# Routing of one prompt block moved in among another block's value tokens, and the cache key units re-dealt 20, 15, 25, 4

## The reference, cut to what matters

```python
q = einsum('td,de->te', xb, w_peer_q)                 # 1024 -> 8 heads x 2 x 128
s = einsum('thpc,hpkc->thpk', q, peer_sub_keys)       # 16 lists of 128 scores
top_s, top_i = top_k(s, 16)                           # per list, then the best 16 of 256 pairs
u = peer_u[expert]                                    # 8 heads x 16 rows of 1024 floats per token
act = gelu(einsum('thkd,td->thk', u, xb))
y = einsum('thk,thkd->td', gate * act, peer_v[expert])
```

## Time and profile before

| what | value |
| --- | --- |
| three runs | 2271.04, 2278.25, 2282.62 us |
| median | 2278.25 us |
| profiled execution, its time | 2283.16 us |
| its span, first to last instruction | 2281.3 us |
| TensorE busy | 1697.5 us (74%) |
| VectorE busy | 1131.0 us (50%) |
| GpSimd busy | 1239.4 us (54%) |
| ScalarE busy | 360.3 us (16%) |
| moved by DMA | 784.77 MB, mean 344 GB/s |
| of it the gathers (GpSimd's queue) | 547.43 MB |
| and SyncE's and ScalarE's transfers (q1) | 231.08 MB |

### The profile page before, as it was taken

One profiled execution on the slowest core, in us unless ns is written; L12 is line 12 of the kernel. 1 busy time (PEld: TensorE's weight loads), 2 busy tenths in 40 slices (PEclk: granted clock), 3 DMA queues, 4 the chain that ended last, 5 costly groups with the idle time before them and its releaser, 6 DMA issues.

```text
span 2281.3 us, 32035 instructions
## 1 busy us (share of the span) xinstructions
PE 1697.5 (74%) x11231; PEld 718.0 (31%) x11231; DVE 1131.0 (50%) x2727; ACT 360.3 (16%) x761; POOL 1239.4 (54%) x1076
## 2 busy tenths in 40 slices
PE   8999898783788767789999777787666223237878
PEld 2455776440112433333334333331212000011212
DVE  2553798988504776482006676780000455550362
ACT  1222243210000222221213222310000000000000
POOL 0000174667777768556668788665233544554765
PEclk9999987897999978899999888899888555557999
DMA  5005495899999999999999999999999999999998
GB/s 226 23 21 186 144 349 184 318 354 346 379 406 394 399 344 398 397 357 399 400 398 390 397 399 399 399 375 368 402 402 401 409 404 404 404 395 368 357 338 330
DMA packets 258555, 784.77 MB, mean 344 GB/s; under 512 B 36593, under 2 KB 45450, under 8 KB 254938
## 3 DMA queue, kind: packets, MB, share of 16 engines
q0 software_dynamic: 150784, 547.43, 62.3%
q1 hardware_dynamic: 106442, 231.08, 27.1%
q10 hardware_dynamic: 1168, 4.23, 0.5%
HBM read 775.80 MB, written 6.81 MB: 343 GB/s over the span
## 4 chain that ended last, share of the span: by engine, by line
DMA 31%; PE 19%; SPq 15%; POOL 8%; issue 8%; DVE 6%; ACT 0%; POOLq 0%; DVEq 0%; ACTq 0%
DMA arena<-peer_v,idxT 15%; DMA arena<-peer_u,eidx 9%; POOL arena L553 8%; SPq L515 7%; PE ps L1931 6%; DMA arena<-vn_pool 5%; SPq L512 4%; SPq L510 4%; PE ps L1993 3%; DVE arena L1370 3%; PE ps L1858 2%; DMA arena<-kpe_pool 2%; PE ps L1733 1%; PE ps L1979 1%; PE ps L1680 1%
## 5 line engine op out<-in xcount | busy, mean ns | idle before, releaser
L553 POOL DMA_INDIRECT arena<-peer_u,eidx x512 | 674.8, 1318 | 616.4 <-PE ps L1847 275.3
L1370 DVE CUSTOM_DVE_ANT_0 arena<-arena 128x1024 f32<-128x1024 f32 x512 | 619.8, 1225 | 684.8 <-DMA arena<-peer_u,eidx 680.8
L553 POOL DMA_INDIRECT arena<-peer_v,idxT x512 | 514.9, 1006 | 391.0 <-PE ps L1931 296.8
L1931 PE MATMUL ps<-arena 128*32 128x512 f32 x2048 | 548.2, 641 | 106.2 <-DMA arena<-peer_v,idxT 102.6
L1993 PE MATMUL ps<-arena 128*128 128x512 f32 x512 | 294.3, 703 | 82.9 <-DMA arena<-kpe_pool 81.0
L2062 PE MATMUL ps<-arena 128*32 128x512 f32 x512 | 105.1, 892 | 265.0 <-DMA arena<-vn_pool 264.5
L1931 PEld LDWEIGHTS ps<-arena 128*32 128x32 f32 x2048 | 104.1, 114 | 427.5 <-DMA arena<-peer_v,idxT 347.7
L895 ACT ACTIVATE arena<-ps 128x512 f32<-128x512 f32 x256 | 152.8, 597 | 516.2 <-PE ps L1993 516.1
L1618 PE MATMUL ps<-arena 128*128 128x512 f32 (+3 forms) x400 | 171.8, 584 | 0.4 <-DVE arena L1033 0.4
L1993 PEld LDWEIGHTS ps<-arena 128*128 128x128 f32 x512 | 96.9, 210 | 208.0 <-issue 115.9
L2062 PEld LDWEIGHTS ps<-arena 128*32 128x32 f32 x512 | 13.2, 127 | 294.6 <-DMA arena<-vn_pool 146.8
(11 more groups left out here) (310 smaller groups left out, 1544.1 us busy)
## 6 DMA issues: line engine op xcount, KB each, us to landing
arena<-kt_pool SPq DMA_DIRECT2D x256, 320.0 KB
arena<-vn_pool SPq DMA_DIRECT2D x256, 320.0 KB
arena<-w_q SPq DMA_DIRECT2D x16, 1024.0 KB, 20.1
arena<-w_in SPq DMA_DIRECT2D x8, 1236.0 KB, 16.0
arena<-w_o SPq DMA_DIRECT2D x16, 512.0 KB, 6.3
arena<-w_q SPq DMA_DIRECT2D x4, 2048.0 KB, 11.1
arena<-peer_u,eidx POOLq DMA_INDIRECT x512
arena<-peer_v,idxT POOLq DMA_INDIRECT x512
```

The costliest lines, as they stand in the source:

```text
L553: pool.indirect_dma_start(ring[:, q % RING, :], None, table, bass.IndirectOffsetOnAxis(ap=index, axis=0)).then_inc(g[q % RING], 16)
L1370: V_.tensor_tensor_reduce(rows, rows, x, 1.0, 0.0, ALU.mult, ALU.add, acc[:, k:k + 1]).then_inc(u_used, 1)
L1931: return T_.matmul(ps[32 * j:32 * j + 32, i, :], W32[:, j, c, :], ring[:, q % RING, 512 * i:512 * i + 512], start=(c == 0), stop=(c == 31) ...
```

## The change

Eight edits, in the order of the diff:

1. The deal of key units: K_U1 20 units instead of 17, K_V1 15 as before, K_U2 25 instead of 28, K_V2 4 as before.
2. A new semaphore dec_rows_in; SyncE loads QS and KS on it as soon as the last query product of block 3 is done (q_ps), ahead of its wait for sc_done. The other four loads stay behind that wait.
3. ScalarE: route_copies(2) stands ahead of gate_exp(1) instead of behind it.
4. VectorE: the two products of decode_queries_1, and its two steps that fill QN, become decode_rows, which needs only QS and KS.
5. The table of block 1's input phase: copy_idxT(1) at dot 12, finish_gates(1) at 16, decode_rows at 38, decode_queries_1 at 43, decode_queries_2 at 49, log_gate_rows at 54, and combine_chunk(0), which stood behind the phase, at 98.
6. query_rows can be issued in two halves of four products.
7. route_beside deals route(2) into 15 pieces: turn_rows, eight halves of query_rows, and six with the transposes and sub-key scores.
8. TensorE: these pieces stand between the value tokens of block 0, at tokens 10, 17, 24 and so on to 108; route(2) is gone from behind that phase, so turn_idx(1) and route(3) follow v_phase(0).

```diff
--- before.py
+++ after.py
@@ -55,7 +55,7 @@
 NU = 2 * NPG
 NCH = 8
 CW = PAST // NCH
-K_U1, K_V1, K_U2, K_V2 = range(0, 17), range(17, 32), range(32, 60), range(60, 64)
+K_U1, K_V1, K_U2, K_V2 = range(0, 20), range(20, 35), range(35, 60), range(60, 64)
 S_U, S_V = 106, 119
 V_V2, V_U3 = range(0, 17), range(17, NPG)
 HPG = [4, 2, 1, 1]
@@ -330,6 +330,7 @@
         v_step = sem("v_step")
         a_step = sem("a_step")
         dec_in = sem("dec_in")
+        dec_rows_in = sem("dec_rows_in")
         k_in = [sem(f"k_in{i}") for i in range(KU)]
         k_used = sem("k_used")
         n_ps = sem("n_ps")
@@ -491,12 +492,13 @@
             sp.wait_ge(h_made, NB)
             sp.dma_start(h_dram[3 * P:4 * P, :], h_of[3]).then_inc(h_stored[3], 16)
 
+            sp.wait_ge(q_ps, 4 * NB)
+            sp.dma_start(QS, qs_dram).then_inc(dec_rows_in, 16)
+            sp.dma_start(KS, ks_dram).then_inc(dec_rows_in, 16)
             sp.wait_ge(sc_done, 4 * NB)
             sp.dma_start(dcon, dec_consts).then_inc(dec_in, 16)
             sp.dma_start(wkd, w_k).then_inc(dec_in, 16)
             sp.dma_start(wkTd, w_kT).then_inc(dec_in, 16)
-            sp.dma_start(QS, qs_dram).then_inc(dec_in, 16)
-            sp.dma_start(KS, ks_dram).then_inc(dec_in, 16)
             sp.dma_start(prow, page_rows).then_inc(dec_in, 16)
             sp.wait_ge(const2_in, 16 * 4)
 
@@ -908,8 +910,8 @@
             route_copies(1)
             gelu(0)
             load_h(0)
+            route_copies(2)
             gate_exp(1)
-            route_copies(2)
             store_y(0)
             route_copies(3)
 
@@ -1304,9 +1306,9 @@
                 dve.wait_ge(idx_ps, b + 1)
                 V_.tensor_copy((idxT if b < NB else idxS)[:, 0:n], ps[:, 7, 0:n]).then_inc(idxT_done, 1)
 
-            def decode_queries_1():
-
-                dve.wait_ge(dec_in, 96)
+            def decode_rows():
+
+                dve.wait_ge(dec_rows_in, 32)
                 m3 = heads(QK[:, 0:H * KM], BD)
                 f3 = heads(QK[:, H * KM:H * KM + 512], BD)
                 qm, km = heads(QS[:, 0:H * KM], BD), heads(KS[:, 0:H * KM], BD)
@@ -1314,13 +1316,19 @@
                 V_.tensor_tensor(m3, qm, km, ALU.mult)
                 step(V_.tensor_tensor(f3, qf[:, :, 0:FD], kf[:, :, 0:FD], ALU.mult))
 
+                V_.tensor_copy(heads(QN[:, 0:512], BD), qf[:, :, 0:FD])
+                V_.tensor_tensor(heads(QN[:, 512:1024], BD), qm[:, :, 0:NOPE], gb(G_KN, BD, H, NOPE), ALU.mult)
+
+            def decode_queries_1():
+
+                dve.wait_ge(dec_in, 64)
+                m3 = heads(QK[:, 0:H * KM], BD)
+                f3 = heads(QK[:, H * KM:H * KM + 512], BD)
                 V_.tensor_reduce(dsm[0:BD, 8:16], m3, AX.X, ALU.add)
                 V_.tensor_reduce(dsm[0:BD, 0:8], f3, AX.X, ALU.add)
                 V_.tensor_copy(dsm[0:BD, 16:24], lf[0:BD, SBLK, :])
                 V_.memset(dsm[0:BD, 24:32], 0.0)
                 V_.memset(dsm[:, 43:44], EPS)
-                V_.tensor_copy(heads(QN[:, 0:512], BD), qf[:, :, 0:FD])
-                V_.tensor_tensor(heads(QN[:, 512:1024], BD), qm[:, :, 0:NOPE], gb(G_KN, BD, H, NOPE), ALU.mult)
                 V_.memset(qz, 0.0)
                 V_.memset(qpz, 0.0)
                 V_.memset(qbd, 0.0).then_inc(dq_done, 1)
@@ -1523,9 +1531,9 @@
             top_subkeys_of(1)
             top_experts(1)
             open_gates(1)
-            u_phase(1, {8: [lambda: add_y(0)], 30: [lambda: copy_idxT(1)], 38: [lambda: finish_gates(1)],
-                        54: [decode_queries_1], 60: [decode_queries_2], 66: [log_gate_rows]})
-            combine_chunk(0)
+            u_phase(1, {8: [lambda: add_y(0)], 12: [lambda: copy_idxT(1)], 16: [lambda: finish_gates(1)],
+                        38: [decode_rows], 43: [decode_queries_1], 49: [decode_queries_2], 54: [log_gate_rows],
+                        98: [lambda: combine_chunk(0)]})
             top_subkeys_of(2)
             top_experts(2)
             open_gates(2)
@@ -1850,14 +1858,15 @@
                 if hi == 4:
                     last.then_inc(q_ps, 1)
 
-            def query_rows(b, i):
-                if i == 0:
+            def query_rows(b, i, lo=0, hi=DC):
+                if i == 0 and lo == 0:
                     pe.wait_ge(xnT2_done, b + 1)
                     pe.wait_ge(wq_in, 16 * DC)
-                for c in range(DC):
+                for c in range(lo, hi):
                     last = T_.matmul(ps[:, RB[b][i], :], xT2[:, c * P:(c + 1) * P], wq[:, c, 512 * i:512 * i + 512],
                                      start=(c == 0), stop=(c == DC - 1))
-                last.then_inc(q_ps, 1)
+                if hi == DC:
+                    last.then_inc(q_ps, 1)
 
             def turn_queries(b, i):
                 pe.wait_ge(qr_done, 4 * (b - 1) + i + 1)
@@ -2105,10 +2114,18 @@
                 if k == 8 * len(K_V2):
                     end_unit(K_V2[-1])
 
+            def route_beside(b, first, every):
+                pieces = [lambda: turn_rows(b), lambda: query_rows(b, 0, 0, 4), lambda: query_rows(b, 0, 4),
+                          lambda: query_rows(b, 1, 0, 4), lambda: query_rows(b, 1, 4), lambda: turn_queries(b, 0),
+                          lambda: query_rows(b, 2, 0, 4), lambda: query_rows(b, 2, 4),
+                          lambda: (turn_queries(b, 1), subkey_scores(b, 0)), lambda: query_rows(b, 3, 0, 4),
+                          lambda: query_rows(b, 3, 4), lambda: (turn_queries(b, 2), subkey_scores(b, 1)),
+                          lambda: turn_queries(b, 3), lambda: subkey_scores(b, 2), lambda: subkey_scores(b, 3)]
+                return {first + every * i: f for i, f in enumerate(pieces)}
+
             route(1)
             turn_w(0)
-            v_phase(0)
-            route(2)
+            v_phase(0, route_beside(2, 10, 7))
             turn_idx(1)
             route(3)
             turn_decode_queries()
```

## The result

| | median, us | runs |
| --- | --- | --- |
| before, same chip | 2280.7 | 6, 2271.04 to 2285.67 |
| after | 2296.45 | 6, 2293.07 to 2298.38 |
| ratio | 1.0072 | 95% interval 1.0055 to 1.0089 |

The change made the kernel 0.7% slower on this chip, by 16 us where 5 us of gain were forecast. On two later chips the same change gave 0.9972 (interval up to 1.0003) and 0.9961 (interval clear of 1). Both need an explanation. Ratios leave out seven executions of all that were made later, because they ran in a slower state of the chip, one of them at 3208 us.

What follows compares the result with a forecast made beforehand. The prediction took the DMA rate as the bound, with only stretches short of 399 GB/s to be won. Its terms, 2 - 7.5 + 0.5 = -5.0 us, took the median of 2278.25 to 2273.3 us, range 2261 to 2290.

Steps and rivals of the forecast that it cites:

- What bounds the kernel: Whole launch: the same bytes must move in any order, so only stretches short of 399 GB/s can be won.
- Part 1: Block 0's value phase: routing 2's pieces among the value tokens cost one loss, +2 us, bounds 0 and 28.
- the rival: Block 0's value phase: pieces starve the ring, costing 15 us (2286 in all) or 28 us (2299); chance 0.13.
- Part 2: Routing 3, waiting for add_y(0), ends near 763 instead of 788 us: 25 us earlier, 10 of 35 lost waiting.
- Part 3: Block 1's input phase, 780 to 840 us: earlier sample queries and first unit fill the gap, -7.5 us, bounds 0 and -7.5.
- Part 4: Three key units moved from U2 to U1: block 1's input phase ends near 980 us, balanced; cost +0.5 us.
- The sum: Whole kernel: 2 - 7.5 + 0.5 = -5.0 us, giving 2273.3 us against the median, 0.22% less.
- The rule weighed behind part 4: HBM to SBUF transfers bound by about 358 GB/s per core: 780 to 840 short by 1.5 us, sum +1 us.

Runs made afterwards that it cites:

- the second pair: The kernel before and the changed kernel, both unchanged, measured again on another chip of the first kind: 2280.45 and 2296.11 us, the latter's ratio 1.0074.
- quarters: The changed kernel with query_rows in pieces of two products every 4 tokens instead of four every 7: 2331.7 us, ratio 0.9990 on a slower chip.

## Why the prediction was wrong

- **What bounds the kernel: right as far as seen.** Most stretches stand at 397 to 409 GB/s before and after, and the whole difference lies in those that don't. That the shortfalls sum to 16.3 us is no test of it: the bytes are the same, so the sum must give the 16.6 us between the two profiles. That the medians differ by 15.8 is in part luck.
- **Part 1, +2 us: the step that failed.** It measured +10.5 us, and +6.7 in the second pair on such a chip. It was mis-sized, and the rival named it: 15 us for a token that costs 1.05 us behind a piece too. That condition was false (22 instructions in 3.91 us is 0.71 a token, as I had taken). The mistake was the next sentence: that the price "falls once or twice and not eight times", for GpSimd would then have buffers in hand. It had them for the three pieces that stand 9 to 10 us behind another, and for no more: the price fell five times, 0.95 to 2.94 us each above 0.3, and four times in the second pair. None of these waits is made good, for GpSimd issues one gather in 1.24 us where TensorE needs one in 1.277; I had written that it recovers 0.04 us a token, and used the figure for the rival alone. The nearest row, 1.89 us, was the price of one piece. Taken for all eight it would have been 13 us, for five 8; I took it once.
- **Part 2, route(3) held by store_y(0): right.** TensorE waited 11.21 us where 10 were forecast. Not forecast was the clock behind it: 0.63 was granted from 732 to 740 us, and the 32 instructions behind the wait took 16.60 us instead of 14.00. The constants were asked for at 769.1, not 765; decode_rows had them in time all the same. A window of after, columns as above:

```profile
732.00:740.00 8.00, 7.31 (x11) 3.14 (x12) 7.58 (x15) 0.64 (x2) 6.23 (x6) 0.63 1.02 412
```

- **Part 3, -7.5 us: right for 780 to 840**, the wait for page_rows too. The first unit came 16.3 us earlier, not 20; decode_queries_1, ahead of dot 43, began at 786.9 instead of 780 to 783. But no 20 us between 765 and 840 were to be below 390 GB/s, and 760 to 780 stood at 348.
- **Part 4, +0.5 us: wrong, the second step that failed.** The phase was to end near 980 with dots and units together. The dots did end as forecast (956.5 against 960). The units were put at 10.4 us each from a start with four landed at 800. But a slot comes free only when TensorE has used its unit, so SyncE issues nothing between the fourth unit (802.7) and 813.8 us, a pause that the earlier trace rows had shown of the old kernel (up to 829.1). At the seventeenth unit the new kernel is only one unit ahead of the old: it begins at 959.7, against 968.1 (the 960.1 in the earlier trace rows is the sixteenth). With 20 units to do instead of 17, four begin behind the last dot where two did. The full ring, with SyncE at one unit in 6.4 us, costs 8.8 us more of DMA time between 960 and 1040. The three units themselves did leave later stretches: block 2's input and value phase together are 553.5 us instead of 564.2, 10.7 less where 9.8 were forecast. But only 2.3 of that lie in the input phase, which was to be 10 us shorter; the rest is in the value phase.
- **The 720 to 780 stretch**, +2.7 us, wasn't in the sum, and the second pair does not show it.
- **The sum.** By the shortfalls, 10.1 - 7.5 + 8.8 + 2.7 + 1.9 (1480 to 1600) is 16.0, in place of 2 - 7.5 + 0.5. Both errors have one root: for each I reasoned with the mean rate of a stretch and not with what the supplier of the transfers may do next. The range's upper end, 2290, took the rival at 15 us and left out that a second loss could come with it.
- **The rule weighed behind part 4**, a bound of 358 GB/s by HBM, would have made the sum +1 us and missed as well. The rows of after show 398 and 399 between 780 and 951 us. The Trainium skill, page "Perfetto Trace Analysis", section "Roofline", says that a core alone can draw more than that share and is then bound by its 16 DMA engines at some 435 GB/s. With that the trace agrees: no slice is above 409, and no window shown above 412.

**What stays open.** What the idleness without a releaser on the second kind of chip is. On TensorE it comes in single waits of up to 31.5 us and in many below 2, and VectorE and ScalarE have it too, with the same program. No run here shows what it is. Then the pieces alone on the first kind, where no run has them without the rest; the price of the new deal and of the store's place apart from each other on the first kind, where only both together were measured (0.7%), and quarters there. Open too is why the tail varies so with one deal: in kernels with pieces and the early start, on the second kind, it is 34 to 39 us with the new deal and 10 to 22 without it.

## What to carry to other kernels

Before work is put among a stream, ask which engine feeds the stream and how much faster than the stream it is. If it has no margin (1.24 against 1.277 us here), each wait that a pause of the consumer puts on it is paid in full, however fast the consumer catches up; here that was five pauses of eight. Where two suppliers share a DMA, look at the end of the phase for which of them will have filled its buffers while the other still has work on an engine: units behind the last dot cost TensorE's time for each, here with the DMA at 230 GB/s instead of 399. And when a change wins in one place and loses in another by some 10 us each, measure it on more than one chip before it is kept.

## What the runs showed of the hardware

- Chips are of two kinds for this kernel: before takes 2280 and 2281 us on two of them and 2333 to 2343 us on four. The slower ones have TensorE idle without a releaser for 34 to 81 us between 540 and 1600 us, in each of fourteen traces, the faster ones for 0 to 0.3. The same change gives 1.007 on the one (twice) and 0.996 and 0.997 on the other. On two of the four slower ones only variants of it were run.
- A gather's issue by GpSimd takes 0.94 us, and up to 3.03 us while VectorE selects experts; in all that adds 4 to 7 us to V0 in twenty traces, with pieces or without.
- TensorE's granted clock was 0.98 in V0 both before and after, and 0.88 and 0.90 in the tail, so the two losses aren't the clock's. Behind 11.21 us of idleness it was 0.63 for 8 us, and 32 products took 16.60 us instead of 14.00.
